# Gated recurrence by products of forget gates in 32-token column groups, with two heads interleaved and the first head's gates made earlier

## The reference

```
log_f = log(lb + (1 - lb) * sigmoid(f));  k = (1 - lb) * sigmoid(-f);  q = silu(q)
b = cumsum(log_f)                         # per chunk, per key channel
decay[t, s] = exp(b[t] - b[s]) for s <= t, else 0
scores[t, s] = sum_c q[t, c] k[s, c] decay[t, s, c]
o[t] = scores[t] @ v + (q[t] * exp(b[t])) @ S
S_new = exp(b[last]) * S + sum_s (k[s] * exp(b[last] - b[s]))^T v[s]
out = rms_norm(o) * gain * silu(gate)
```

## Time and profile before

| what | us |
|---|---|
| median of three runs | 2214.31 |
| the profiled execution | 2216.99 |
| its span | 2215.2 |
| mean granted clock of TensorE | 0.931 |
| PE busy in the span | 1968.1 (89%) |
| VectorE busy | 933.5 (42%) |
| ScalarE busy | 546.9 (25%) |
| GpSimd busy | 645.7 (29%) |

### The profile page before, as it was taken

The page is one execution under the profiler, slowest core; times in us unless marked ns, Lnnn a source line. Parts: engine busy times, 40 slices in busy tenths (PEclk is TensorE's granted clock), DMA queues, the critical chain, the costliest instruction groups (busy, mean ns, idle before and its releaser), DMA issues. The chain is left out here.

```text
span 2215.2 us, 29001 instructions
## 1 busy us (share of the span) xinstructions
PE 1968.1 (89%) x10290; PEld 1584.4 (72%) x10290; DVE 933.5 (42%) x1537; ACT 546.9 (25%) x1126; POOL 645.7 (29%) x556
## 2 busy tenths in 40 slices
PE   6999999878777883788699999999999859999998
PEld 5788997844443553676588999888788636777776
DVE  3550001077776446975345444211000035656564
ACT  4210110155555334332232000000011132323231
POOL 3322222055555003642305222332222032212120
PEclk9999999978888995778799999999999969999999
DMA  4332222143421454021543322332222197656553
GB/s 150 94 111 80 89 79 70 51 136 124 123 85 34 131 177 165 11 62 60 182 149 114 99 79 79 119 107 87 83 84 69 45 259 215 214 167 200 189 165 119
DMA packets 207956, 257.93 MB, mean 116 GB/s; under 512 B 22756, under 2 KB 149412, under 8 KB 207588
## 3 DMA queue, kind: packets, MB, share of 16 engines
q1 hardware_dynamic: 152164, 197.69, 28.9%
q10 hardware_dynamic: 53680, 53.50, 7.4%
q0 software_dynamic: 2000, 5.25, 0.7%
HBM read 174.85 MB, written 79.17 MB: 115 GB/s over the span
## 5 line engine op out<-in xcount | busy, mean ns | idle before, releaser
L342 PE MATMUL odd_bank<-odd_w_hi,odd_h_hi 128*128 128x512 f32 x576 | 224.9, 391 | 2.5 <-DVE odd_shared L679 2.5
L342 PE MATMUL odd_bank<-odd_w_lo,odd_h_hi 128*128 128x512 f32 x576 | 224.8, 390 | 0.0
L342 PE MATMUL odd_bank<-odd_w_hi,odd_h_lo 128*128 128x512 f32 x512 | 200.0, 391 | 0.0
L290 POOL CAST odd_w_hi<-odd_raw 128x1024 fp32r<-128x1024 f32 x48 | 51.2, 1068 | 337.6 <-PE odd_bank L342 316.5
L342 PE MATMUL even_bank<-even_h_hi,even_w_hi 128*128 128x362 f32 (+1 forms) x384 | 127.7, 332 | 4.5 <-DVE even_stage_tm L679 4.5
L342 PE MATMUL odd_bank<-odd_h_hi,odd_w_hi 128*128 128x362 f32 (+1 forms) x384 | 126.1, 328 | 1.8 <-POOL odd_w_lo L292 1.8
L342 PE MATMUL even_bank<-even_h_lo,even_w_hi 128*128 128x362 f32 (+1 forms) x384 | 127.1, 331 | 0.0
L342 PEld LDWEIGHTS odd_bank<-odd_w_hi,odd_h_hi 128*128 128x128 f32 x576 | 108.5, 188 | 25.4 <-DVE odd_shared L679 2.9
L342 PE MATMUL even_bank<-even_h_hi,even_w_lo 128*128 128x362 f32 (+1 forms) x384 | 126.6, 330 | 0.0
L342 PE MATMUL odd_bank<-odd_h_lo,odd_w_hi 128*128 128x362 f32 (+1 forms) x384 | 126.1, 328 | 0.0
L342 PE MATMUL odd_bank<-odd_h_hi,odd_w_lo 128*128 128x362 f32 (+1 forms) x384 | 125.1, 326 | 0.0
(11 more groups left out here) (300 smaller groups left out, 4430.7 us busy)
## 6 DMA issues: line engine op xcount, KB each, us to landing
odd_raw<-in_w_in_odd SPq DMA_DIRECT2D x48, 512.0 KB, 3.7
even_raw<-in_w_in_even SPq DMA_DIRECT2D x32, 512.0 KB, 3.8
k_page<-in_cache_k SPq DMA_DIRECT2D x64, 256.0 KB, 3.0
v_page<-in_cache_v SPq DMA_DIRECT2D x64, 256.0 KB, 3.0
rt_s<-in_state_ret SPq DMA_DIRECT2D x32, 512.0 KB, 5.8
out_ret_sample<-rt_s SPq DMA_DIRECT2D x32, 512.0 KB, 3.2
v_tm<-odd_shared ACTq DMA_DIRECT2D x64, 128.0 KB, 1.9
g_tm<-odd_shared ACTq DMA_DIRECT2D x64, 128.0 KB, 1.9
```

Source lines behind the costliest of these rows:

```text
L290: nc.gpsimd.tensor_copy(hi, r).then_inc(w_hi_done, 1)
L342: mm = pe.matmul(out, stationary, moving, start=(j == 0), stop=(j == len(pairs) - 1))
```

## The change

Forget gates are never turned into logs. A level's decay is a product of gates, and because levels now go from small blocks to large, each level needs only products of pairs of the level before.

- The "plain" segment stores sigmoid(f) and sigmoid(-f), two rows of 1088 per feature row.
- f = lb + (1 - lb) sigmoid(f) and k = (1 - lb) sigmoid(-f) are two ScalarE instructions per head (`gates`). GpSimd makes q*f and seven halving pair products (544 down to 8 elements, `products`).
- Level 0 is the diagonal (k with q), level 1 neighbours (k with q*f), and from there keys and queries are multiplied **in place** by the product of the other half-block (`move`, VectorE, two instructions of 544 or 512 elements). After the last level the keys hold the decay to the chunk's end, so the separate product for the state is not needed.
- Levels 0 to 5 need only blocks of 32 tokens: four matmuls of 32x32 per chunk in four column groups, one masked copy of 128x256 into `picks`. Level 6 uses two column groups, level 7 one 64x64 block; ScalarE copies those into `scores`.
- `order` interleaves two heads, head h + 1 four levels behind head h. `rest(h - 2)` is spread over these levels; in head 3's last four levels `rest(2)` takes two steps per level; `rest(3)` comes alone. Transposes and sample updates get two banks, the mix is stored in two pieces, and all four heads have their own values, states and gates, loaded at the start.
- Head 0's loads, gates and products, the bounds (by exp, add, reciprocal) and the masks go into the samples' attention (`FirstHead`), in memory shared with the prompt's attention (`place`); the loops of ScalarE and VectorE there are written out.

```diff
@@ project_in, ScalarE
+                if kind == "plain":
+                    ...
+                    for i in range(2):
+                        if g == 0:
+                            act.wait_ge(left_fm[i], 16 * (at["fm"] // 2 + row) + 16)
+                        ins = nc.scalar.activation(stage_fm[:, i, g0:g0 + gn], src[:, 0:gn], ACT.Sigmoid, scale=-1.0 if i else 1.0)
+                    ins.then_inc(free, 1)
+                    if g == 2:
+                        act.wait_ge(free, this + NBANK)
+                        act.dma_start(place(row), stage_fm[:, 0, :]).then_inc(left_fm[0], 16)
+                        act.dma_start(negative[row * P:row * P + P, :], stage_fm[:, 1, :]).then_inc(left_fm[1], 16)
@@ FirstHead
+    def gates(self, nc, h, f, k):
+        nc.scalar.activation(f, f, ACT.Identity, scale=self.om[:, h:h + 1], bias=self.lb[:, h:h + 1]).then_inc(self.f_done, 1)
+        nc.scalar.activation(k, k, ACT.Copy, scale=self.om[:, h:h + 1]).then_inc(self.k_done, 1)
+    def products(self, nc, pool, h, q, f, qd, e):
+        nc.gpsimd.tensor_tensor(qd, q, f, ALU.mult).then_inc(self.qd_done, 1)
+        for j in range(self.NM):
+            out = self.blocks(f, e, j + 1)
+            pairs = self.blocks(f, e, j)[:, 0:2 * out.shape[1]].rearrange("p (c two) -> p c two", two=2)
+            if j:
+                pool.wait_ge(self.e_done, self.NM * h + j)
+            nc.gpsimd.tensor_tensor(out, pairs[:, :, 0], pairs[:, :, 1], ALU.mult).then_inc(self.e_done, 1)
@@ attend_samples
+            first.load(sp)                                  # SP, before the first value rows
+            pool.wait_ge(first.q_in, 16)                    # GpSimd, after its last copy
+            pool.wait_ge(first.f_done, 1)
+            first.products(nc, pool, 0, first.q, first.f, first.qd, first.e)
...
+                if it == NTURN - 1:                         # ScalarE, between weights(it, 0) and weights(it, 1)
+                    act.wait_ge(first.prep, 5)
+                    act.wait_ge(first.f_in, 16)
+                    act.wait_ge(first.k_in, 16)
+                    first.gates(nc, 0, first.f, first.k)
@@ hgrn, order
+        order = [(h, s - APART * h) for s in range(APART * (HB - 1) + NLEV) for h in range(HB) if 0 <= s - APART * h < NLEV]
+            for h, i in order:
+                alone = h == HB - 1 and i >= APART
+                if h >= 2 and i == 0 or alone and i == APART:
+                    for _ in now:
+                        pass
+                    now = rest(h - 1 if alone else h - 2)
+                level(h, i)
+                next(now, None)
+                if alone:
+                    next(now, None)
@@ hgrn, VectorE
+            def move(h, j):
+                kk, qq = halves(k[h], j), halves(qd[h], j)
+                dve.wait_ge(scored, nth[h, j + 1] + 1)
+                dve.wait_ge(e_done, NM * h + j)
+                dve.tensor_tensor(kk[:, :, 0, :], kk[:, :, 0, :], decays(h, j, 1), ALU.mult).then_inc(k_moved, 1)
+                dve.tensor_tensor(qq[:, :, 1, :], qq[:, :, 1, :], decays(h, j, 0), ALU.mult).then_inc(q_moved, 1)
+            def level(h, i):
+                if i >= 1:
+                    move(h, i - 1)
+                if i < NPICK:
+                    pick(h, i)
@@ hgrn, TensorE
+                    pe.wait_ge(k_moved, nth_move[h, i - 2] + 1)
+                    pe.wait_ge(q_moved, nth_move[h, i - 2] + 1)
+                lhs, rhs = k[h], qd[h] if i else q[h]
+                if i < NPICK:
+                    ...
+                    for c in range(NCH + 1 if i < NSAMPLE else NCH):
+                        for g in range(4 if c < NCH else 2):
+                            tok = slice(c * P + 32 * g, c * P + 32 * g + 32)
+                            mm = pe.matmul(near[n % 2][32 * g:32 * g + 32, c, :], lhs[:, tok], rhs[:, tok], start=True, stop=True,
+                                           skip_group_check=True, tile_position=(0, 32 * g))
```

More of the change, by code:

```diff
@@ L519, in act_unit @@
                 s = u // 6
-                if kind in ("silu", "plain"):
+                if kind == "plain":
+                    f, g = j // 3, j % 3
+                    row = 2 * s + f
+                    g0, gn = GROUPS[g]
+                    act.wait_ge(full, this)
+                    for i in range(2):
[7 more added lines that the diff above has]
+                        act.dma_start(negative[row * P:row * P + P, :], stage_fm[:, 1, :]).then_inc(left_fm[1], 16)
+                if kind == "silu":
                     f, g = j // 3, j % 3
@@ L1303, in copy_weights @@
                 nc.scalar.copy(wT[:, 0:4, :], turn[0][:]).then_inc(held_a, 1)
-            with act.Fori(0, NTURN) as it:
+            for it in range(NTURN):
                 parts = iter(())
@@ L1493, in run, with halves, decays, outputs_of @@
                 pass
+            for _ in rest(HB - 1):
+                pass
+        def halves(t, j):
+            n = T if j < 3 else TP
+            return t[:, 0:n].rearrange("p (c two m) -> p c two m", two=2, m=1 << j)
+        def decays(h, j, half):
+            n = (T if j < 3 else TP) >> j + 1
+            return first.blocks(f[h], e[h], j)[:, 0:2 * n].rearrange("p (c two) -> p c two", two=2)[:, :, half:half + 1].to_broadcast([P, n, 1 << j])
+        def outputs_of(g):
+            if g < NG:
+                return o[g][:].rearrange("p c n -> p (c n)"), (ku[0][:].rearrange("p c n -> p (c n)") if g else ss[:]), slice(4 * P * g, 4 * P * (g + 1))
+            return ss[:, 0:TS], ss[:, TS:2 * TS], slice(TP, T)
         @block.sync
@@ new lines, in level @@
+            def level(h, i):
+                if i == 0 and h + 1 < HB:
+                    act.wait_ge(sig_in[h + 1], 16)
+                    act.wait_ge(neg_in[h + 1], 16)
+                    first.gates(nc, h + 1, f[h + 1][:], k[h + 1][:])
+                if i == NLEV - 1:
+                    s = scores[h % 2]
+                    if h == 0:
+                        act.wait_ge(zeroed, 4)
+                    if h >= 2:
+                        act.wait_ge(o_done, 3 * (h - 1))
+                    act.wait_ge(scored, nth[h, NLEV - 2] + 1)
+                    for part, at in ((96, 0), (64, 64)):
+                        nc.scalar.copy(s[at:at + 32, :, at + 32:at + 64], far[part:part + 32, :, 0:32]).then_inc(far_read, 1)
@@ L1652, in rest @@
                 scales(h, 2)
[L1654 to L1657 removed]
+            run(level, rest)
         @block.vector
         def _(dve):
[L1661 to L1666 removed]
@@ L1817, in rest @@
[L1817 to L1823 removed]
+                    pe.wait_ge(s1_done, NG * h)
+                for g in range(NG):
+                    if h and g:
+                        pe.wait_ge(ln_done, 3 * h - 1)
+                    for c in range(4):
@@ L1882, in rest @@
                 yield
-                sums(NG)
-            run(scores_slot, rest)
+                sums(h, NG)
+            run(level, rest)
 def project_out(nc, tag, mix_fm, weight, x_of, y_of):
```

560 lines of the change are left out of this document (249 added, 311 removed).

## The result

The changed kernel takes 2127.29 us (median of four runs, 2125.09 to 2128.96) against 2215.61: ratio 0.960, interval 0.958 to 0.963, 88 us less. I had said 2141, in 2112 to 2178. The range held it and the direction was right; the size was short by 15 us.

The account below looks back on a forecast made before the run. VectorE, 88% busy, was taken to bound the recurrence, PE close behind. The order's terms summed to 147 us, starting the next stage some 74 us earlier; less 1.5 in the samples, -73: median 2141 us, range 2112 to 2178.

Parts of the forecast that it names:

- The bound: Recurrence: VectorE sets the loop, PE close behind; after the change some 22 us of VectorE per head against 39.
- two full periods: Recurrence, two periods of four pairs of levels plus the rest of heads 0 and 1: 31 us each, 62.
- The largest certain item: Start of the recurrence: with head 0 prepared early, PE begins about 1 us after the barrier instead of 24.8: -24 us.
- Samples: Samples' attention: head 0's loads, gates and products placed there add 1.5 us (0 to 4).
- PE per head: Recurrence: 20 ns per small matmul, near level 1.4 us at full clock, twice at the low; 27.8 us per head.
- changes of the tiling mode: Recurrence, PE: 16 changes per head with about 0.2 us of idle each, 3.2 us per head.
- The sum of the order: Recurrence: times of the interleaved levels and rests in order, together 147 us from its start to the last store.
- four pairs: Recurrence, four pairs of levels of heads 0 and 1: 21 us with the first stall, PE at the low clock.
- last rest: End of the recurrence, head 3's rest alone: 23 us instead of 25.6, two banks taking away waits.
- Nothing given back: Stage after the recurrence: starts as before with a cold PE and full DMA, so no gain is lost there.
- VectorE beside GpSimd: Recurrence: contention with 10 us of GpSimd work per head costs VectorE 2.5 us per head.
- My second rival: Recurrence: GpSimd excludes VectorE for its whole time, +7.5 us per head, 2161 us in all; chance 10%.

Follow-up runs that it names:

- The fourfold copies: Changed kernel with each masked copy of 128x256 made four times, same result: 2140.9 us, ratio 0.9658 to the kernel before.
- the edit that removes the overlap: Changed kernel with GpSimd starting head 0's products only after VectorE's last running sum of the samples: 2120.7 us, ratio 0.9565 to the kernel before.
- heads in turn: Changed kernel without interleaving: all eight levels of one head, then the next, with the previous head's rest spread over them: 2131.1 us, ratio 0.9597.
- the run with wide weights: Changed kernel with a near level's 68 matmuls made 18, 128 key columns by 32 query columns per chunk: 2174.4 us, ratio 0.9797.
- the groups ran in turn: Changed kernel with a near level's two loops swapped, all matmuls of one 32-column group one after another: 2138.7 us, ratio 0.9646.

## Why the prediction was right, and where it was short

**The bound.** Right that VectorE set the loop and that halving its work moves it. It needed 85.3 us; I had 22 per head, 88. The fourfold copies show that its work still counts by half. Right too that PE would then stand beside it: in the two full periods PE was busy for 44.9 of 55.6 us, VectorE for 39.8.

**Start.** Predicted 24 us, got 24.6 at PE. But the prediction gave it all to preparing head 0 early. Gates and products at the start cost the recurrence nothing, loads too 6.5 us. "The largest certain item" came mostly from a gate chain without log, running sum and exp.

**Samples.** +1.5 predicted, 3.1 measured, inside the stated 0 to 4. The step that was short: the prediction set GpSimd's products beside the chain and saw the 0.6 us of slack, but gave no working for the 1.5 and did not ask what a running sum costs beside GpSimd. It took 2.3 us more, and the edit that removes the overlap gives the 3.3 us back.

**PE per head.** Mis-sized, the largest error. A near level takes 0.73 us at full clock (from 900.67 to 901.40, below) and 1.07 at the low one (two in 2.13 at the start), against 1.4 and 2.8: 11 ns per instruction at 2.4 GHz, below my lower end of 14, and 16 ns at 1.2 GHz. Doubling at the low clock was wrong too; it was half as much again. The 0.7 us per near level at full clock that I had too much, six levels and the far ones, is some 5 us per head.

The 3.2 us per head for changes of the tiling mode were too much as well. I had read 0.2 us of idle at each off the weight loads; PE shows about half of that. At full clock two instructions of 0.11 us are followed after 0.22 us where the mode stays, and after 0.32 us where it changes to 64 columns. Out of a near level the next instruction starts 0.13 us after the last one, where inside it 9 ns lie between two:

```profile
963.55 0.39 PE L1907 MATMUL hg_o<-hg_qd,hg_state 128*128 128x128 f32 x2
963.77 1.02 PE L1865 MATMUL hg_ss<-hg_sq,hg_ones 128*128 128x512 f32 x2
...
897.37 0.39 PE L1907 MATMUL hg_o<-first_place,hg_state 128*128 128x128 f32 x2
897.69 1.15 PE L1858 MATMUL hg_far<-hg_qd,hg_k 128*64 128x64 f32 x16
...
900.67 0.80 PE L1845 MATMUL hg_near<-hg_qd,hg_k 128*32 128x32 f32 x68
901.40 0.43 PE L1920 MATMUL hg_ss<-hg_scores_s,hg_v 64*128 64x64 f32 x2
```

The Trainium skill (TensorEngine Tiling (Array Packing), Key Properties) says that a change of tiling mode drains the engine; these 0.1 us agree with it.

**The sum of the order.** Predicted and measured, in us: head 0 alone 15, 12.7; four pairs 21, 22.8; two full periods 62, 55.6; head 3's last levels 26, 22.6; last rest 23, 16.6; all 147, 130.3. The four pairs were over although PE was busy for 10.0 us in them against 22.4 in my sum: waits took that. Mid-level pauses of PE (below) and moves beside GpSimd stand there. The last rest is the largest miss for its length. It took 25.6 us before at a clock of 0.67; after, the clock in its 20 us was 0.91, and two of the waits were gone by the second banks. I had carried the low clock over.

**Interleaving.** My sum was built on it; heads in turn are within 2 us. So the sum does not show that interleaving was needed, and no run shows what it is worth at the same clock.

**Nothing given back.** Right, 1153.3 and 1153.4 us behind it.

**VectorE beside GpSimd.** I had put 2.5 us per head on it, 10 in all. The 56 moves lost 9 to 10 us: 48.7 in sum against 38.6 at 0.69 each. The loss is not spread: ten moves took 0.93 to 2.38 us, each began inside a GpSimd multiplication and ended 0.54 to 0.61 us after it; the other 46 took 0.67 to 0.73, also those beside which GpSimd began a multiplication later. The Trainium skill (SBUF — State Buffer, the section SBUF: two separate sides) has the two exclude each other for whole instructions; the single moves and the running sum (4.64 for 2.31 us) agree. My second rival read that rule as the whole of GpSimd's time, 10 us per head; it falls due only where a move meets a multiplication that is already running.

## What to carry to other kernels

Where only blocks near the diagonal are wanted, fp32 matmuls with 32-column weights in interleaved column groups cost a small fraction of full ones: 11 ns against 0.12 us each at full clock, 0.73 against 2.0 us for a level, though it needs four times as many. Of the 91 us that the stage lost, the run with wide weights puts 48 on them, with VectorE's work already down. The rest came with less work on VectorE and a shorter chain to the first matmul; no run has narrow weights without the new algebra, where VectorE at 88% would have been in the way. Take work off the engines that are full before planning clever orders: interleaving and the early start were worth 2 and, net, about 3 us or nothing. Work moved under another stage must be checked against what runs beside it there: "idle" GpSimd time cost VectorE's chain 3 us.

## What the runs showed of the hardware

PE pauses inside a level, with no semaphore between the matmuls, each 126 to 127 matmul instructions: after 180, 307, 434, 561 and 687 of them. Timeline of PE, changed kernel:

```profile
857.14 0.65 PE L1845 MATMUL hg_near<-first_place 128*32 128x32 f32 x30 [0.94 <-DVE hg_picks L1763]
860.99 0.69 PE L1845 MATMUL hg_near<-first_place 128*32 128x32 f32 x33 [3.20 <-issue]
...
863.26 0.88 PE L1853 MATMUL hg_far<-first_place 128*32 128x32 f32 x25 [0.66 <-DVE first_place L1753]
865.93 0.32 PE L1853 MATMUL hg_far<-first_place 128*32 128x32 f32 x4 [1.80 <-issue]
```

With a weight load each, 127 matmuls are close to 256 instructions, and the instruction queue moves pieces of 16 KB:

```profile
q8 instruction: 80, 1.31, 0.3%
```

So they look like PE running out of its instruction stream, and the trace has the packets of that queue, with start and duration. Changed kernel, in us:

| pause of PE | packet of 16 KB that landed last | from landing to PE's start |
|---|---|---|
| 844.36 to 846.00 | 843.68 to 844.69 | 1.31 |
| 853.27 to 854.65 | 852.11 to 853.07 | 1.58 |
| 857.79 to 860.99 | 858.46 to 859.62 | 1.38 |
| 864.14 to 865.93 | 863.29 to 864.48 | 1.45 |
| 870.45 to 870.84 | 868.34 to 869.53 | 1.31 |
| 876.89 to 878.58 | 876.39 to 877.31 | 1.27 |
| 907.23 to 908.20 | 905.37 to 906.71 | 1.49 |

Each pause ends 1.3 to 1.6 us after such a packet has landed. The same holds, with 1.2 to 1.6 us, for the 57 pauses of this kind in the other kernels, so PE waits for its instructions there. The pauses last 0.4 to 3.2 us and sum to some 11 us; all but the last sit in the first 40 us. Their length goes by how late the packet starts. The longest one here is the only one whose packet started after PE had stopped. Why a packet starts late is open: DMA was full in that pause and at the start of the one of 4.98 us, but no run varies that alone. What the pauses cost the stage is open too, since heads in turn, with 3.3 us of them, took no less time.

The granted clock stayed at 0.50 for the first 40 us of the changed recurrence, where PE was busy 16.6 of 40 us, and was 0.77 and 0.88 in the same stretches when the groups ran in turn and PE was busy 25.1 (rows above): a slower form of the same matmuls got the faster clock.
